# Residual rows in the order of the expert weights, the norm factor applied per slot, and no token turns between router and experts

## What is computed

```python
x = x + mixing_block(rmsnorm(x, norm_mix), ...)         # projections w_in (2048 x 5120) and w_out (2048 x 2048)
x = x + cross_attention(rmsnorm(x, norm_xattn), k, v, w_q, w_o)
t = rmsnorm(x, norm_moe)                                # hierarchical MoE
g = argmax(t @ router_group_w + bias)                   # one expert group of 4
i = top_k(softmax((t @ router_expert_w + bias)[g]), 2)  # two of its 4 experts
x = x + sum(gate * (silu(t @ w_gate[e]) * (t @ w_up[e])) @ w_down[e])    # w_gate, w_up: 2048 x 512
y = rmsnorm(x, norm_final)
```

## Time and profile before

| what | value |
| --- | --- |
| median of 3 runs | 1483.22 us |
| the profiled execution | 1484.51 us, its span 1482.8 us |
| TensorE matmul / weight load busy | 1427.7 us (96%) / 1089.8 us (73%) |
| VectorE, ScalarE, GpSimd busy | 555.9, 190.1, 796.8 us |
| chain that ended last, by engine | TensorE 83%, DMA 10%, VectorE 3%, ScalarE 2% |
| chain, by line | L840 40%, L897 13%, L1184 11%, tiles of w_up 8% |
| bytes moved | 377.07 MB, 254 GB/s on average |

### The profile page before, as it was taken

One profiled execution on the slowest core, in us unless ns is written; L12 is line 12 of the kernel. 1 busy time (PEld: TensorE's weight loads), 2 busy tenths in 40 slices (PEclk: granted clock), 3 DMA queues, 4 the chain that ended last, 5 costly groups with the idle time before them and its releaser, 6 DMA issues.

```text
span 1482.8 us, 25563 instructions
## 1 busy us (share of the span) xinstructions
PE 1427.7 (96%) x9308; PEld 1089.8 (73%) x9308; DVE 555.9 (37%) x1067; ACT 190.1 (13%) x392; POOL 796.8 (54%) x1453
## 2 busy tenths in 40 slices
PE   6999999999999999999999999979999999999997
PEld 6999999998889999998777799963334334344344
DVE  3546578829575342222111342151112122122123
ACT  5100321000000010003222200051000000000003
POOL 3777587979987757763444467512451440522500
PEclk8999999999999999999999999989999999999999
DMA  8344344445654444464788744747999999999993
GB/s 256 124 161 142 107 150 129 155 145 176 208 167 162 142 166 143 146 236 191 299 318 310 248 152 154 293 189 323 421 421 422 422 422 422 422 422 422 422 422 140
DMA packets 106120, 377.07 MB, mean 254 GB/s; under 512 B 12421, under 2 KB 12421, under 8 KB 76290
## 3 DMA queue, kind: packets, MB, share of 16 engines
q1 hardware_dynamic: 103778, 371.68, 65.8%
q10 hardware_dynamic: 2272, 4.42, 0.9%
HBM read 369.30 MB, written 6.77 MB: 254 GB/s over the span
## 4 chain that ended last, share of the span: by engine, by line
PE 83%; DMA 10%; DVE 3%; ACT 2%; issue 1%; SPq 1%; POOL 0%; POOLq 0%; ACTq 0%; DVEq 0%
PE ps L840 40%; PE ps L897 13%; PE ps L1184 11%; DMA tiles<-in_expert_w_up 8%; PE ps L1250 4%; PE ps L1214 3%; PE ps L966 2%; DMA tiles<-in_expert_w_down 2%; PE ps L790 1%; PE ps L1201 1%; PE ps L984 1%; PE ps L974 1%; PE ps L1005 1%; DMA A<-in_norm_final 1%; PE ps L1032 0%
## 5 line engine op out<-in xcount | busy, mean ns | idle before, releaser
L749 POOL COPY A<-A 128x16 f32 x952 | 146.1, 213 | 289.4 <-issue 289.3
L840 PE MATMUL ps<-hT,tiles 128*128 128x144 f32 x1792 | 295.3, 288 | 3.4 <-ACT A L1406 1.5
L840 PE MATMUL ps<-A,tiles 128*128 128x144 f32 x1792 | 262.0, 286 | 0.8 <-DVE A L2003 0.7
L840 PEld LDWEIGHTS ps<-hT,tiles 128*128 128x128 f32 x1792 | 251.6, 191 | 5.0 <-issue 2.6
L840 PEld LDWEIGHTS ps<-A,tiles 128*128 128x128 f32 x1792 | 237.0, 190 | 1.9 <-DVE A L2003 0.9
L702 POOL TENSOR_TENSOR tiles<-tiles 128x512 f32<-128x512 f32 x88 | 117.3, 1333 | 173.4 <-DMA tiles<-in_w_in 70.4
L840 PE MATMUL ps<-tiles 128*128 128x144 f32 x960 | 171.1, 287 | 0.0
L1184 PE MATMUL ps<-tiles,A 128*64 128x512 f32 x512 | 147.0, 601 | 13.2 <-DMA A<-in_expert_w_up 6.4
L840 PEld LDWEIGHTS ps<-tiles 128*128 128x128 f32 x960 | 140.4, 191 | 0.0
L897 PE MATMUL ps<-tiles,mT 128*128 128x256 f32 x512 | 132.9, 382 | 1.0 <-ACT kv_stage L1440 1.0
L1709 DVE COPY pair_sums<-ps 128x144 f32<-128x144 f32 x44 | 13.5, 308 | 300.4 <-PE ps L840 300.4
(11 more groups left out here) (350 smaller groups left out, 1698.6 us busy)
## 6 DMA issues: line engine op xcount, KB each, us to landing
tiles<-in_expert_w_down SPq DMA_DIRECT2D x56, 1024.0 KB, 22.4
tiles<-in_w_in SPq DMA_DIRECT2D x40, 1024.0 KB, 5.1
tiles<-in_expert_w_gate SPq DMA_DIRECT2D x32, 1024.0 KB, 22.1
tiles<-in_expert_w_up SPq DMA_DIRECT2D x32, 1024.0 KB, 22.5
A<-in_expert_w_up SPq DMA_DIRECT2D x24, 1024.0 KB, 25.2
tiles<-in_xa_w_k SPq DMA_DIRECT2D x16, 1024.0 KB, 5.1
tiles<-in_w_out SPq DMA_DIRECT2D x16, 1024.0 KB, 5.1
tiles<-in_xa_w_q SPq DMA_DIRECT2D x16, 1024.0 KB, 5.1
```

What stands on the lines that cost most here:

```text
L749: m = nc.gpsimd.tensor_copy(xe[:, :, at + n:at + n + 1], h_moe_or_zero[:, :, bass.ds(token, 1)])
L840: return mm(one(u + mp, x, TH), w[:, kp, mp, :], rhs, start=(first and g == 0 and kp == 0), stop=(g == 3 and kp == 1), skip_group_check=True)
```

## The change

The residual's rows are kept in the order in which the gate and up tiles are read. `e_gate` and `e_up` become "e (g p k) f -> e g p k f", so partition p of block 4 g + k is row 512 g + 4 p + k; w_in, w_q and the router weights are loaded in the same way (`turned_tiles_of`, the router weights in eight DMAs instead of two), the input x is transposed by taking every fourth column (`fourths`), w_out and w_o are cut so that their output columns come in that order, and the scatter and the final output undo it. The gain rows that belong to the residual are transposed a second time in that order. hT itself is gathered into `xe`, and all turns of tokens, `h_moe`, `h_tok` and the zero column go. The factor 1/rms is no longer in the gathered rows: TensorE picks it for each slot (`take_roots`), ScalarE gives it to Silu as scale, and the gate value is multiplied with it once more for the up half. Tiles 12 and 13 lie in the space of the attention output and load when w_o is done. Slots without a token read token 0.

```diff
-for _n, _c in (("norm_mix", 2), ("norm_xattn", 2), ("norm_mem", 2), ("norm_moe", 2), ("rg_conv_w", CW),
+for _n, _c in (("norm_mix", 2), ("norm_xattn", 2), ("norm_moe", 2), ("norm_final", 2), ("norm_mem", 2), ("rg_conv_w", CW),
+TURNED = ROWS["norm_mem"]
-        vec = sb("vec", [P, GB, NROWS])
+        vec = sb("vec", [P, GB, NROWS + TURNED])
+        def fourths(x, b):
+            return x.rearrange("p (g n k) -> p g k n", k=KT, n=P)[:, b // KT, b % KT, :]
-        def quarter_blocks(t):
-            w = tile_of(t).rearrange("p (kp kk) (mp mm n) -> p kk mm kp mp n", kk=2, mp=2, mm=2)
+        def quarter_blocks(name, t):
+            w = tile_of(t)
+            if name in ("w_out", "w_o"):
+                w = w.rearrange("p (kp kk) (n mp mm) -> p kk mm kp mp n", kk=2, mp=2, mm=2)
+            else:
+                w = w.rearrange("p (kp kk) (mp mm n) -> p kk mm kp mp n", kk=2, mp=2, mm=2)
-        e_gate = a["expert_w_gate"][0].rearrange("e (p g k) f -> e g p k f", k=KT, p=P)
+        e_gate = a["expert_w_gate"][0].rearrange("e (g p k) f -> e g p k f", k=KT, p=P)
```

On SyncE's queue, and the wait ahead of GpSimd's gather:

```diff
-            sp.dma_start(wr[:, :, 0:NG], a["router_group_w"][0].rearrange("(b p) g -> p b g", p=P)).then_inc(wr_loaded, 16)
+            for g in range(KT):
+                sp.dma_start(wr[:, KT * g:KT * g + KT, 0:NG], w_route[0][g]).then_inc(wr_loaded, 16)
+                sp.dma_start(wr[:, KT * g:KT * g + KT, NG:NG + NE], w_route[1][g]).then_inc(wr_loaded, 16)
                 elif m >= 12:
-                    after_event(sp, EVENT["h_tok_rest"] + 1)
+                    sp.wait_ge(tile_used, TILE["moe"])
...
-            pool.wait_ge(h_moe_out, 3)
+            pool.wait_ge(h_ready, 4 * HREADY["moe"] + 4)
```

On TensorE; the three matmuls of the counts, which stood ahead of the slot numbers, come behind `take_roots`:

```diff
+                m = nc.tensor.transpose(bank(u, b // 4)[:, at + NROWS:at + NROWS + TURNED], fourths(pack[0:TURNED, :], b),
+                                        ident[0:TURNED, 0:TURNED])
-                turn_scaled(UNIT["h"] + c, x_nat[0:rows, c, :], diag[0:rows, c, 0:rows], rows)
+                turn_scaled(UNIT["h"] + c, lambda b: fourths(x_nat[0:rows, c, :], b), diag[0:rows, c, 0:rows], rows)
-            turn_tokens(0, range(12))
-            turn_back_chunk(0, UNIT["h_moe"])
+            def take_roots(out):
+                for s in range(2):
+                    for c in range(3):
+                        n = own_rows[c]
+                        m = mm(out[:, s:s + 1], pick[0:n, c, C * s:C * s + C], h_rstd[0:n, c:c + 1], start=(c == 0), stop=(c == 2))
+            pe.wait_ge(tokens_numbered, 1)
+            pe.wait_ge(pick_ready, 1)
+            number_slots(first_slot_sums)
+            take_roots(first_slot_roots).then_inc(unit_done, 1)
 ...
-            turn_back_chunk(1, UNIT["h_moe_rest"])
-            turn_back(2, lambda b: bank(UNIT["places"], 0)[:, b * NB * ST:(b + 1) * NB * ST])
-            pe.wait_ge(h_moe_out, 3)
             read_out(pe, UNIT["places"])
```

On ScalarE; both of its gathers stand between the wait for `h_ready` and the copy of the roots:

```diff
-            for c in range(3):
-                tokens_out(c)
             slots_numbered(first_slot_sums, EVENT["pick_0"], None, 0)
+            act.wait_ge(h_ready, 4 * HREADY["moe"] + 4)
...
+            after_event(act, EVENT["root_0"])
+            roots_out(first_slot_roots)
+            act.wait_ge(slot_root_out, 1)
+            act.sem_inc(half_free[u % 2], 1)
-                fn(silu[0:C, :], ps[0:C, 4 + s, :], ACT.Silu).then_inc(silu_ready, 1)
+                fn(silu[0:C, :], ps[0:C, 4 + s, :], ACT.Silu, scale=slot_root[0:C, s:s + 1]).then_inc(silu_ready, 1)
```

On VectorE:

```diff
             after_event(dve, EVENT["counts"])
-            v.tensor_copy(tab[:, 0, :], bank(u, 3)[:, 0:NE]).then_inc(half_free[u % 2], 2)
+            v.tensor_copy(tab[:, 0, :], bank(u, 3)[:, 0:NE]).then_inc(half_free[u % 2], 1)
+            then(tt(G(11), G(11), h_rstd[:, 0:3].unsqueeze(2).broadcast_to([P, 3, 4]), ALU.mult))
```

## The result

| what | before | after |
| --- | --- | --- |
| median | 1483.33 us (1483.09 to 1485.98, 4 runs) | 1611.12 us (1609.5 to 1612.85, 4 runs) |
| ratio | | 1.0857, 95% interval 1.0838 to 1.0876 |
| span of the profiled execution | 1482.8 us | 1611.1 us |

The change costs 128 us, nearly 9%. The prediction said 1482.8 us with a range to 1540, so the time lies far outside; the direction had 0.43. In the kernel after, L862 is the old L840, L805 the old L790 (scaled transposes of x), L790 the old L775 (plain transposes), L815 and L816 the transposes of the parameter rows, L721 to L726 the old L702 to L707, L1192 the old L1184, L765 the old L749.

A forecast was written before the change was run, and what follows sets the result against it. Bound taken: TensorE ahead of the experts, then DMA engines at 422 GB/s. Terms -1.6 + 1.0 + 0.2 = -0.4 us, strided reads 0, gave 1482.8 us on the median; range 1479 to 1540, the forecast's own 1480.3 to 1486.

The forecast's parts named there:

- that row: VectorE's L2083: 16 elements read 16 B apart in 172 ns, against 170 for neighbours; strided reads taken as 0.
- the ends: Strided reads of w_out, w_o and x: TensorE 0 to +114 us; GpSimd 0 to +32 us.
- Weight loads slow: Rival: w_out and w_o bound by strided weight loads above 0.1225 us; 1532 at 1.5 times, 1597 at twice; chance 0.26.
- a rule that spoke against the change: Trainium skill, on SBUF reads: 16-byte lines, full bandwidth needs at least two accesses to a line.
- near twice: Part of the slow-weight-load rival: strided loads in w_out and w_o cost about twice, 1597 us; chance 0.14.
- slower from 7.09 us a tile: Rival: GpSimd's strided additions bound w_out and w_o above 7.09 us a tile; 1486 to 1515 us; chance 0.17.
- Parameter transposes: At the start: eight more transposes for the gain rows in both orders, +1.0 us.
- Router to experts: Between router and first expert matmul: missing turns gain 0.5 to 3.1 us, taken as -1.6 us.
- the slow ends: First expert matmul at half clock: 998.1 by ScalarE's release, 998.7 by VectorE's gather, against 999.24 us before.
- the router loads: Ahead of the w_o loads in SyncE's queue: six more router DMAs, 0.33 us each, 2 us, hidden.
- the two regimes: Ahead of the experts TensorE time is kernel time; afterwards the end follows the first expert load behind the prefetched ones.
- the first branch: From first expert matmul to the first expert load behind the prefetched ones: at half clock before and after.

The follow-up runs named there:

- the two moves: In the kernel without 16-byte steps: counting matmuls ahead of the slot numbers, and ScalarE's copy of the slot roots between its two gathers; 1481.55 us.
- the kernel without steps: The changed kernel with w_out, w_o, x, parameter rows, y_pair and output all in runs, no 16-byte steps, rows mixed up; 1486.6 us.
- the grouped kernel: The kernel without 16-byte steps, with counts and root copy moved earlier, plus the eight small gain-row transposes behind the eight of 71 rows; 1480.18 us.

## Why the prediction was wrong

**The step that failed** is one sentence: "I take 0 for both, by that row, and keep the ends." The ends were right. At the upper one, "twice, 0.22", it put 3.1 us a tile, 98 us for both matrices and 16 at the start; measured were 0.233 us a pass, 3.53 us a tile, 113 us over 32 tiles, and 11 at the start, as the table of stretches shows; with TensorE alone strided the kernel takes 1609.5 us, nearly all of it. The rival "Weight loads slow ... at twice 1597" is what happened, at 2.1 times the load of 0.11 us. The mechanism was described as it is ("bound by loads of strided weights as soon as one takes over 0.1225 us"); the choice between the ends was wrong. (The differences 0.0955 and 0.041 us a pass should be 0.0975 and 0.0425; that moves no time by 2 us.)

**Why the row misled.** L2083 is VectorE reading 16 elements in 172 ns. Nearly all of this is a fixed cost, for an operation on 3 elements takes as long in the same stretch of the kernel before:

```profile
989.83 0.17 DVE L2114 TENSOR_TENSOR mT<-mT 128x3 f32<-128x3 f32 x1
```

Had each element cost twice as much, 16 of them would hardly have shown in that row. Nor does VectorE read a row in 0.11 us per 128 elements, as a weight load does. Such a row bounds nothing, and with a margin of 12% the only rows near in kind, the weight loads, were silent. What was left was a rule that spoke against the change, and the prediction gave near twice 0.14 and drew the range at 1540, leaving it out. With no row of the same engine and operation, the range should have been kept to 1597.

**GpSimd.** Taken as 0; its additions grew by 1.2 us a tile to 6.4, inside the 7.09 allowed, and the predicted bound "slower from 7.09 us a tile" was not reached (6.98 at most, beside VectorE). The estimate from "GPSIMD Engine Reference" in the Trainium skill, section 7, 7.7 us a tile, was high: 6.4 measured. Yet alone it costs 12.5 us, not 0. The bound looked at who waits for GpSimd's sums and at a steady tile; it left out that VectorE works beside GpSimd at the heads of w_out and w_o and is slowed by it.

**Parameter transposes.** +1.0 predicted, +3.2 measured: eight more at the rate of the earlier trace rows is right only if they stand together (2.1 us for sixteen), and not in alternation.

**Router to experts.** -1.6 predicted, -0.05 measured. The mechanisms were the named ones, ScalarE's release behind both gathers and VectorE's late counts, and the granted clock was 0.50, the half level, as chosen. From the masks (1109.54) to the slot numbers (1116.24) are 6.7 us, predicted 6.8. From there to the first expert product are 10.2, predicted 8.8, and here a row was misread. The sentence "its two gathers run from 993.76 to 1002.13, 8.4 us" takes the last row for the end of the gathers, but that view was cut at 1002 us and shows 2 of 16 copies. The same row in a wider window:

```profile
1001.79 2.02 ACT L1567 COPY A<-A 128x16 f32 x16 [0.51 <-issue]
```

The gathers lasted to 1003.81, 10.05 us, and after the change they take 10.03 (1116.24 to 1126.27). With 10.05 for 8.4 the same sum gives 989.3 + 10.05 + 0.4 = 999.75 at the half level: no gain, as measured. Besides, the -1.6 was more than the slow ends of the prediction's own sum gave (998.1 and 998.7 against 999.24). Because both ends had been named, the two moves worth 5 us were plain.

**The rest.** `take_roots` in the loops, tiles 12 and 13, the router loads (each takes about 0.65 us of the queue, not 0.33 as taken from the earlier trace rows, but hidden all the same) and the rate of 422 GB/s came out as said. The first expert product moved by 127.18 us, the first expert load behind the prefetched ones from 1008.03 to 1136.06, by 128.03, and the end by 128.3: the two regimes added up as said. The 0.85 us between the first two are the first branch, which was not "paid at the half level before and after": in its first 5 us the granted clock was 0.67 before and 0.52 after.

## What to carry to other kernels

Before a layout makes TensorE load float32 weights at a step, look at the margin between the length of a pass and that of its weight load: here a step of 8 bytes was free and one of 16 nearly doubled the pass, 0.1225 to 0.233 us. Price an unknown access pattern by a row of the same engine and a long enough operation; a short operation is all fixed cost and proves nothing. A row that ends at the edge of its window may go on behind it; look at the next stretch before you take its end. Where several engines release one instruction, removing work pays only after each late release has been moved.

## What the runs showed of the hardware that was not expected

- A pass of 128 float32 weights, 144 columns: 0.1225 us in runs and at 8 bytes, 0.233 at 16 bytes, 0.238 at 32 ((169.10 - 166.48) / 512 = 0.005 more).
- The price does not go with the granted clock. The scaled transposes of x at 16-byte steps take 0.233 us from start to start at the full level (25.4 to 34 us) and at the half (35.6 to 41.8 us); without steps, in the kernel before, 0.112 at the full level and 0.213 at the half. The windows of the kernel after, then of the kernel before (length, then TensorE's passes; a pass that crosses an edge counts in full; the clock is the third number from the end):

```profile
25.40:34.00 8.60, 8.60 (x39) 8.60 (x38) 1.51 (x3) 2.18 (x8) 2.54 (x3) 1.00 0.68 149
35.60:41.80 6.20, 6.20 (x28) 6.20 (x28) 0.28 (x1) 1.23 (x5) 0.00 (x0) 0.50 0.00 0
```

```profile
16.90:19.10 2.20, 2.20 (x12) 2.20 (x12) 0.49 (x1) 0.00 (x0) 1.27 (x2) 0.50 1.05 387
19.50:24.70 5.20, 5.20 (x49) 5.20 (x48) 2.53 (x3) 2.18 (x8) 5.04 (x5) 1.00 1.05 408
```

- So where TensorE runs at the half level the steps cost little or nothing: sixteen plain transposes of x, with weights at 16-byte steps, had their loads in 3.29 us at 0.50 (42.15 us), and in the kernel without steps, also at 0.50, in 3.27; without steps at the full level (the grouped kernel) in 1.73.
- VectorE beside a GpSimd that never pauses: one operation for each of GpSimd's additions, in the four shown each ends 0.31 or 0.32 us behind one. Four operations of 128x288 took 7.12 us instead of 1.80.
- GpSimd at 16-byte steps: 2.11 us for the first addition of a tile against 1.27, 1.12 to 1.53 for the other three, 6.4 for the tile against 5.15. The second addition reads two strided operands like the first and takes 1.12; why is open. At 8 bytes the first takes 1.50.
- Expert tiles of 1 MB in pieces of 8 KB or one stretch: 422 GB/s; gate and up tiles in 4 KB: 413 to 415; in 2 KB: 395 to 401, with the DMA engines just as busy.
- Transposes of 71 and 8 rows in alternation: 0.53 us a pair; grouped: 0.26.
